# MLA: a head's keys projected between its predecessor's third and fourth scores, its queries two heads early

## What is computed

```python
cq = (rms_norm(m_q, p['mla_q_norm']) @ p['mla_w_qb']).reshape(B, S, MLA_HEADS, MLA_NOPE + MLA_ROPE)
q_nope, q_rope = cq[..., :MLA_NOPE], cq[..., MLA_NOPE:]          # 64 + 32 columns a head
q_rope = apply_rope(q_rope, rope32)                               # latent tokens only
kv = (ckv_all @ p['mla_w_kvb']).reshape(B, Sk, MLA_HEADS, MLA_NOPE + MLA_V)
k_m = concatenate([kv[..., :MLA_NOPE], broadcast(kr_all)], axis=-1)
o_mla = softmax_attention(concatenate([q_nope, q_rope]), k_m, kv[..., MLA_NOPE:], scale)
```

## Time and profile before

| what | value |
|---|---|
| median of 3 runs | 3044.15 us (3044.12 to 3048.35) |
| the profiled execution | 3046.05 us, its span 3044.3 us |
| PE busy | 2801.6 us, 92% of the span |
| DVE busy | 2017.5 us, 66% |
| ACT busy | 1648.3 us, 54% |
| POOL busy | 265.4 us, 9% |
| MLA loop of the first layer | from 400.15 us, some 120 us; the second layer's from 1884.96 us |

### The profile page before, as it was taken

The page is one execution under the profiler, slowest core; times in us unless marked ns, Lnnn a source line. Parts: engine busy times, 40 slices in busy tenths (PEclk is TensorE's granted clock), DMA queues, the critical chain, the costliest instruction groups (busy, mean ns, idle before and its releaser), DMA issues.

```text
span 3044.3 us, 45368 instructions
## 1 busy us (share of the span) xinstructions
PE 2801.6 (92%) x16026; PEld 2206.6 (72%) x16026; DVE 2017.5 (66%) x3103; ACT 1648.3 (54%) x2435; POOL 265.4 (9%) x294
## 2 busy tenths in 40 slices
PE   6989988999989999999988898999998899999995
PEld 3868956988947777777657796588897677777774
DVE  3463256464469999999835524654645799999994
ACT  3263344253248777777634524432624677777774
POOL 0050012020010000000002300210201000000000
PEclk9999999999989999999999999999999899999997
DMA  7102100222379999999821021013043799999991
GB/s 294 63 29 91 60 29 29 84 72 78 124 278 355 336 336 337 336 335 337 307 72 63 29 96 57 1 56 128 29 146 132 263 336 337 337 334 339 333 344 70
DMA packets 280124, 564.13 MB, mean 185 GB/s; under 512 B 14041, under 2 KB 19873, under 8 KB 279329
## 3 DMA queue, kind: packets, MB, share of 16 engines
q1 hardware_dynamic: 273056, 543.25, 50.1%
q10 hardware_dynamic: 4448, 9.87, 0.9%
q0 software_dynamic: 2464, 8.91, 0.8%
HBM read 546.36 MB, written 15.63 MB: 185 GB/s over the span
## 4 chain that ended last, share of the span: by engine, by line
PE 66%; DVE 16%; ACT 6%; issue 5%; ACTq 2%; DVEq 1%; DMA 1%; POOL 0%; SPq 0%; POOLq 0%
PE mm L1035 23%; PE mm L1553 19%; DVE w_lo L2128 7%; PE mm L1058 6%; PE mm L1088 2%; DVE x L2136 2%; ACTq L2049 2%; DVE scratch L2355 1%; ACT w_hi L1631 1%; PE mm L1277 1%; PE oo L992 1%; ACT scratch L1631 1%; DVE scratch L2128 1%; PE mm L953 1%; ACT pt L1631 1%
## 5 line engine op out<-in xcount | busy, mean ns | idle before, releaser
L2128 DVE TENSOR_TENSOR w_lo<-ring,w_hi 128x1024 fp32r<-128x1024 f32 x768 | 912.3, 1219 | 86.8 <-ACT w_hi L1631 69.8
L1631 ACT ACTIVATE w_hi<-ring 128x1024 fp32r<-128x1024 f32 x768 | 803.4, 1059 | 278.5 <-PE mm L1553 255.9
L1035 PE MATMUL mm<-h_hi,ring_lo 128*128 128x320 f32 (+1 forms) x1344 | 313.0, 314 | 2.5 <-DVE h_lo L2128 2.0
L1035 PEld LDWEIGHTS mm<-h_hi,ring_lo 128*128 128x128 f32 (+1 forms) x1344 | 222.8, 188 | 16.3 <-issue 14.4
L1553 PE MATMUL mm<-w_lo,xa_hi 128*80 128x512 f32 x512 | 205.2, 401 | 18.2 <-DVE w_lo L2128 11.8
L2128 DVE TENSOR_TENSOR ring_lo<-ring,dw_hi 128x512 fp32r<-128x512 f32 (+1 forms) x104 | 70.0, 676 | 206.2 <-ACT dw_hi L1631 205.2
L1553 PE MATMUL mm<-w_lo,xb_hi 128*128 128x512 f32 x512 | 203.8, 398 | 0.0
L1553 PE MATMUL mm<-w_hi,xa_lo 128*80 128x512 f32 x512 | 202.9, 396 | 0.0
L1553 PE MATMUL mm<-w_hi,xa_hi 128*80 128x512 f32 x512 | 201.8, 394 | 0.0
L1553 PE MATMUL mm<-w_hi,xb_hi 128*128 128x512 f32 x512 | 199.8, 390 | 0.0
L1553 PE MATMUL mm<-w_hi,xb_lo 128*128 128x512 f32 x512 | 199.3, 389 | 0.0
(11 more groups left out here) (323 smaller groups left out, 6030.9 us busy)
## 6 DMA issues: line engine op xcount, KB each, us to landing
ring<-in_w_ff SPq DMA_DIRECT2D x384, 1024.0 KB, 6.4
ring<-in_w_ada SPq DMA_DIRECT2D x48, 1024.0 KB, 7.4
ring<-in_w_gate SPq DMA_DIRECT2D x24, 1024.0 KB, 5.7
ring<-in_w_in SPq DMA_DIRECT2D x16, 1024.0 KB, 9.3
ring<-in_w_o SPq DMA_DIRECT2D x8, 1024.0 KB, 7.8
x_spill<-x SPq DMA_DIRECT2D x2, 2560.0 KB, 12.8
ring<-in_w_br_da SPq DMA_DIRECT2D x4, 1024.0 KB, 6.3
ring<-in_w_br_mla SPq DMA_DIRECT2D x4, 1024.0 KB, 6.2
```

What stands on the lines that cost most here:

```text
L1035: last = pe.matmul(out[0:width, lo:hi], w_, h_[:, k, lo:hi], start=(k == 0 and i == 0), stop=(k == KT - 1 and i == 2))
L1631: return act.activation(out, in_, ACT.Copy, scale=scale)
L2128: return dve.tensor_tensor(out, in0, in1, op)
```

## The change

Three orders move together. On PE (and for ACT's `head_in`), K of head h+1 stands between S2 and S3 of head h, and Q of head h+2 stands behind the short S4 of head h; Q of head 1 is written ahead of the loop. The turn numbers come from a generator of the same order, instead of a formula. On DVE the three rope parts stand two steps earlier: rope0 at the end of step t = 0, rope1 at the end of step t = 1, and rope2 in step t = 2 ahead of M2.

```diff
+def _mla_order():
+    yield from (("prep", 0, 0), ("prep", 0, 1), ("prep", 1, 0))
+    for i in range(MLA_N):
+        h, t = divmod(i, TT)
+        if t == PRT - 1 and h < MH - 1:
+            yield "prep", h + 1, 1
+        yield "s", i
+        if t == PRT and h < MH - 2:
+            yield "prep", h + 2, 0
...
 PE:
                 for piece in range(2):
                     project_head(0, piece)
+                project_head(1, 0)
...
-                    if 1 <= t <= 2 and hd < MH - 1:
-                        project_head(hd + 1, t - 1)
+                    if t == PRT - 1 and hd < MH - 1:
+                        project_head(hd + 1, 1)
...
                     last.then_inc(mm_full[j % 2], 1)
+                    if t == PRT and hd < MH - 2:
+                        project_head(hd + 2, 0)
...
 ACT:
-                        if 1 <= t <= 2 and hd < MH - 1:
-                            head_in(hd + 1, t - 1)
+                        if t == PRT - 1 and hd < MH - 1:
+                            head_in(hd + 1, 1)
...
+                        if t == PRT and hd < MH - 2:
+                            head_in(hd + 2, 0)
...
 DVE:
-                    if t == 4 and hd < MH - 1:
+                    if t == 2 and hd < MH - 1:
                         rope_head(hd + 1, 2)
...
-                    if t in (2, 3) and hd < MH - 1:
-                        rope_head(hd + 1, t - 2)
+                    if t in (0, 1) and hd < MH - 1:
+                        rope_head(hd + 1, t)
```

More of the change, by code:

```diff
@@ L328, in job_turn @@
     return MM["pairs"] + q
+def _mla_order():
[7 more added lines that the diff above has]
+            yield "prep", h + 2, 0
+MLA_AT = {what: n for n, what in enumerate(_mla_order())}
+assert len(MLA_AT) == MLA_N + 2 * MH
 def mla_s(i):
-    h, t = divmod(i, TT)
-    return MM["mla_heads"] + 2 + h * (TT + 2) + t + (min(t, 2) if h < MH - 1 else 0)
+    return MM["mla_heads"] + MLA_AT["s", i]
 def mla_prep(h, piece):
-    return MM["mla_heads"] + (piece if h == 0 else 2 + (h - 1) * (TT + 2) + 1 + 2 * piece)
+    return MM["mla_heads"] + MLA_AT["prep", h, piece]
 def t_order(n, per_tile, every):
@@ L1878, in _ @@
                 head_in(0, 1)
+                head_in(1, 0)
                 def mla_turn_even(i):
```

## The result

| kernel | median, us | runs |
|---|---|---|
| before | 3044.94 (3043.50 to 3048.35) | 20 |
| with the change | 3049.82 (3047.00 to 3051.62) | 20 |

The ratio is 1.0014, with a 95% interval of 1.0008 to 1.0020: a small loss of 2.4 to 6.1 us, 4.9 us by the medians. The forecast was 5.8 us, a time of 3049.95. Of the three outcomes that were given a chance, it is the one with 0.50, a loss of less than 6.1 us.

The account below looks back on a forecast made before the run. PE was taken to bound the two MLA loops. Per head, waits of 1.57 us go and some 2.3 come; 2.93 us a layer, 5.8 of both, puts the 3044.15 median at 3049.95 us, range 3046.0 to 3055.0.

Parts of the forecast that it names:

- S3: Fourth score product of a steady head on PE: starts at 9.35 us, held by DVE's chain, 0.26 behind PE's own offer.
- Q: Queries' projection on PE in a steady head: starts at 12.55 us after waiting about 1 us for ACT's exp.
- M2: Third maximum of a steady head on DVE, behind the rope parts: starts at 7.53 us.
- V4': Values product on PE in a steady head: starts at 6.70 us, with a new wait of some 0.95 for ACT's copy.
- S0 to M1: From a steady head's first score product on PE to its second maximum on DVE: 4.42 us, 1.33 late through rope0.
- DVE's step behind an M: Start-to-start distance on DVE from a maximum to the next instruction: 0.85 us, 0.82 of it the maximum and 0.03 handoff.
- From Q to V1: On PE, from the queries' projection to the values product behind it: 2.16 or 2.32 us, taken as 2.24.
- The sum: Loss over all heads of a layer: 1.42 + 3.45 - 1.64 - 0.3 = 2.93 us, of both layers 5.8.
- PE's own path: PE's own work in a steady head of the kernel before: 14.38 us, the 15.95 period without 1.57 of waits.
- The free Q: Head 1's queries' projection ahead of the loop costs nothing: its 2.32 us lie within PE's 2.40 wait for the rope.
- The faster one: Rival: the rope holds up no maximum and only PE's order counts; period 15.44 us, time 3033.3 us, chance 0.10.
- The collision of DVE and POOL: Rival: a POOL instruction holds up rope1 on DVE; 6.9 us more, 12.7 in all, time 3056.8 us, chance 0.05.

Follow-up runs that it names:

- run with the rope back: Against the changed kernel: the three rope parts returned to their old places, projections left as in the change; 3033.05 us, ratio 0.9963.
- run without waits: Against the changed kernel: queries' projection moved ahead of the short last scores, rope0 and rope1 at end of step 2, rope2 in step 4; 3018.29 us.

## Why the prediction held

**The sign and the size.** The forecast of 5.8 us lay at the upper side of the measured interval of 2.4 to 6.1; the medians differ by 4.9. Its mechanism is the one the trace shows: V4' waits 0.94 us for a P4' that stands behind a late E1, S3 is released by E2, Q waits 1.09 for E3. The runs with the rope moved show it to be the cause.

**The walk through a head.** The steps came out within 0.22 us, but each was a little early in the trace. S0 to M1: 4.42 forecast, 4.32 measured (446.79 to 451.11). M2: 7.53, measured 7.32. V4' 6.70, measured 6.48. S3: 9.35, measured 9.14. Q: 12.55, measured 12.34. The term that was too large is DVE's step behind an M: I had 0.85 us, and it is 0.74 behind M0 and 0.73 behind M1 in this head; V4' also came 0.33 behind the start of P4', and not 0.43. PE by itself would have offered S3 at 8.97 (V4' 6.48, K 1.06 and S3 1.43 behind it), so DVE's chain beats it by 0.17 and not 0.26. From Q to V1 I took 2.24 between the ends 2.16 and 2.32, and it was 2.33, the upper end. The errors partly cancel: 12.34, 2.33 and 1.84 make 16.51. S3 has no bracket, though it starts 1.60 behind K and not 1.43, 0.96 behind E2 (454.97), as the chain had it; in the heads of 16.65 us the trace gives it a wait of 0.23. Periods by starts of S0 in the first layer: 15.54, 16.84, 16.64, 16.51, 16.65, 16.51, 14.11, against 15.42, five times 16.64, 14.31. The five steady heads of this layer make 83.15 us where the forecast has 83.20, closer than the walk deserves: one of them, of 16.84, has a delay that the walk knows nothing of (see the end). In the second layer the five make 82.83.

**The sum.** From the first head's S0 to the last head's is 112.80 us in the first layer with the change (397.77 to 510.57), and was 109.67 (400.15 to 509.82): 3.13 more; 2.82 more in the second layer (112.47 against 109.65). The last head gave 0.37 back in the first layer (16.50 from its S0 to its last T, where it was 16.87); I had said 0.3. With the same in the second layer that is 5.2 us, where the sum said 5.86.

**PE's own path.** I put PE's own work at 14.38 us, by taking the waits out of the period. The run without waits has 14.08. So the stage had 1.9 us a head to win, and not 1.57. The brackets were too small: from S0 to an unhindered T3' is 1.08 us (446.79 to 447.87), and I had left 1.24 there after taking the 0.29 of T3' out.

**The free Q.** The Q of head 1 ahead of the loop cost nothing, as said. The first Q of the layer moved by 2.39 us between the two profiled executions, and S0 by 2.38.

**The rivals.** The faster one, by which the rope would hold nothing up, had 3033.3 us; it did not occur. The run with the rope back comes to the same state by another way (M1 and M2 on time, the projections moved): it has a period of 15.35 us where the rival had 15.44, and took 3033.05. That the two times agree within 0.3 us is partly luck, since the kernel before had 3045.28 beside it and not 3044.15. The collision of DVE and POOL did not decide: W0 ends at 452.09, 0.35 us ahead of rope1 at 452.44 (I had put the slack at 0.44), and W1, which starts inside rope2 at 453.40, is the one that gets longer, while rope2 lasts 0.68 as always.

```profile
451.29 0.80 POOL L887 TENSOR_SCALAR scratch<-scratch,stat 128x640 f32<-128x640 f32 x1 [3.86 <-DVE stat L2484]
453.46 1.29 POOL L887 TENSOR_SCALAR scratch<-scratch,stat 128x640 f32<-128x640 f32 x1 [1.37 <-DVE stat L2484]
```

The Trainium skill, SBUF — State Buffer, section "Who interferes with whom", says that issue order decides who blocks. This trace agrees: rope2 starts 0.06 ahead of W1, and W1 takes 0.49 longer. A DVE instruction that loses was not seen in any run here: in the MLA loops of all ten traces no product or sum of the rope lasts over 0.68 us.

## What to carry to other kernels

When work is moved out of a place, ask what it covered there: Q and K among the first scores gave DVE and ACT the time for M1 and E1, and a stretch that is emptied must not be filled on the next engine at once. With two PSUM tensors in turn, a product waits for the reader of the turn two ahead, so a long product should follow the turn that is read early, and the short one should take the turn that is read late: that alone (Q ahead of S4) was worth 14 us here. Walk one period of all engines with start-to-start distances from the trace; it gave the sign of a change of 0.16%, and found the order that is 0.9% better.

## What the runs showed that I had not expected

- DVE's start-to-start distance behind an M of the same shape is not fixed. Behind M0 it is 0.74 or 0.75 us in every steady head; behind M1 it is 0.73 in one head (451.11 to 451.84) and 0.83 in the next (467.63 to 468.46), and behind M2 0.74 and 0.85 in the same heads. Periods alternate between 16.51 and 16.65 us with it. I took 0.85 throughout. What sets it was not tried and stays open.
- From Q to the next product it is 2.16 us or 2.33 (459.13 to 461.46). The 0.17 go with the loading of Q's first weights and not with a wait as such: where it is 2.16 the load starts 0.10 us ahead of Q (448.04 for 448.14), where it is 2.33 the load starts with Q (459.13). The first Q of the layer, which has no wait in the trace, shows the same: load and Q at 391.54, the next product 2.33 later. Scores and values that waited cost nothing more: from S3 to T1 it is 1.18 us after a wait of 0.23 (472.57 to 473.75) and without one (455.93 to 457.11).
- The first of the steady heads took 16.84 us, 0.2 to 0.3 more than the others, in the first layer only; V4' waits 1.25 us there. The delay arises on DVE: its M1 comes 0.39 us behind the start of R, where it is 0.07 or 0.08 in the next heads, with 0.22 us of idle time that waits for nothing the profile shows:

```profile
417.94 0.82 DVE L2285 TENSOR_REDUCE stat<-mm 128x1 f32<-128x640 f32 x1 [0.22 <-issue]
```

The same gap of 0.22 us, ahead of the M1 of the second head in the first layer alone, is in the traces of all four kernels that have rope0 at step 0, and in none of the other six. Why stays open.
